# Layer norm from early moments, two weight units prepared ahead, and products that nobody reads

## The reference

```
def layernorm(x, g, b):
    mu = jnp.mean(xf, -1, keepdims=True)
    var = jnp.mean(jnp.square(xf - mu), -1, keepdims=True)
    return ((xf - mu) * lax.rsqrt(var + LN_EPS) * g + b).astype(x.dtype)

x = layernorm(ALPHA * x + part(x), g, b)        # four times, ALPHA = sqrt(2), LN_EPS = 1e-5
swiglu = (silu(x @ wg) * (x @ wu)) @ wd         # wg, wu: 1024 x 2816, wd: 2816 x 1024
```

## Time and profile before

| what | value |
|---|---|
| three runs shown | 1865.67, 1865.85, 1878.34 us, median 1865.85 |
| the profiled execution | 1866.61 us, of it the span of the core 1865.0 us |
| mean granted clock of TensorE | 0.926 of full speed |
| PE busy | 1659.9 us, 89% of the span |
| PEld, DVE, ACT, POOL busy | 81%, 40%, 35%, 13% |
| moved by DMA | 132.40 MB, mean 71 GB/s |

### The profile page before, as it was taken

One profiled execution on the slowest core, in us unless ns is written; L12 is line 12 of the kernel. 1 busy time (PEld: TensorE's weight loads), 2 busy tenths in 40 slices (PEclk: granted clock), 3 DMA queues, 4 the chain that ended last, 5 costly groups with the idle time before them and its releaser, 6 DMA issues. The chain is left out here.

```text
span 1865.0 us, 31270 instructions
## 1 busy us (share of the span) xinstructions
PE 1659.9 (89%) x12319; PEld 1511.7 (81%) x12321; DVE 750.9 (40%) x1433; ACT 648.4 (35%) x1274; POOL 241.7 (13%) x345
## 2 busy tenths in 40 slices
PE   8995297889999899979956899998687999998996
PEld 7994167789999899869945567766587999998994
DVE  4325963443333322265336554443435333332224
ACT  4424262242222211165326554454315222221113
POOL 1002530110000000010042333331021000000000
PEclk9997598889999999989978699999798999999998
DMA  6332102213223233133342121001312233223321
GB/s 158 91 80 55 31 1 70 67 57 90 82 86 90 76 94 93 40 59 88 83 130 58 46 79 57 1 1 42 96 55 63 87 90 90 84 74 96 91 62 48
DMA packets 253288, 132.40 MB, mean 71 GB/s; under 512 B 45142, under 2 KB 252106, under 8 KB 253002
## 3 DMA queue, kind: packets, MB, share of 16 engines
q1 hardware_dynamic: 251402, 127.39, 24.6%
q0 software_dynamic: 1792, 3.76, 0.7%
HBM read 124.81 MB, written 10.43 MB: 73 GB/s over the span
## 5 line engine op out<-in xcount | busy, mean ns | idle before, releaser
L210 PE MATMUL ps<-x_hi,w_hi 128*128 128x272 f32 x2288 | 476.2, 289 | 4.6 <-DVEq L575 4.2
L214 PE MATMUL ps<-x_hi,w_lo 128*128 128x272 f32 x2288 | 474.9, 289 | 0.0
L212 PE MATMUL ps<-x_lo,w_hi 128*128 128x272 f32 x2288 | 473.2, 288 | 0.0
L227 DVE TENSOR_TENSOR w_lo<-w_raw,w_hi 128x1024 fp32r<-128x1024 f32 (+1 forms) x167 | 226.3, 1355 | 491.5 <-ACT w_hi L220 491.5
L220 ACT ACTIVATE w_hi<-w_raw 128x1024 fp32r<-128x1024 f32 (+1 forms) x179 | 199.8, 1116 | 640.6 <-PE ps L214 633.9
L210 PEld LDWEIGHTS ps<-x_hi,w_hi 128*128 128x128 f32 x2288 | 361.0, 189 | 7.0 <-DVEq L575 4.8
L212 PEld LDWEIGHTS ps<-x_lo,w_hi 128*128 128x128 f32 x2288 | 361.0, 189 | 0.0
L214 PEld LDWEIGHTS ps<-x_hi,w_lo 128*128 128x128 f32 x2288 | 358.7, 190 | 0.0
L210 PE MATMUL ps<-h_hi,w_hi 128*128 128x272 f32 x704 | 147.9, 292 | 9.7 <-DVEq L785 9.7
L214 PE MATMUL ps<-h_hi,w_lo 128*128 128x272 f32 x704 | 147.5, 291 | 0.0
L212 PE MATMUL ps<-h_lo,w_hi 128*128 128x272 f32 x704 | 147.1, 291 | 0.0
(11 more groups left out here) (392 smaller groups left out, 2052.7 us busy)
## 6 DMA issues: line engine op xcount, KB each, us to landing
w_raw<-in_ffn_w_gate SPq DMA_DIRECT2D x44, 512.0 KB, 3.8
w_raw<-in_ffn_w_up SPq DMA_DIRECT2D x44, 512.0 KB, 3.8
w_raw<-in_ffn_w_down SPq DMA_DIRECT2D x32, 704.0 KB, 4.7
w_raw<-in_ab_w_in SPq DMA_DIRECT2D x17, 512.0 KB, 4.2
w_raw<-in_c_w_in SPq DMA_DIRECT2D x13, 512.0 KB, 3.8
w_raw<-in_c_w_in SPq DMA_DIRECT2D x16, 256.0 KB, 3.9
w_raw<-in_c_w_out SPq DMA_DIRECT2D x32, 128.0 KB, 3.1
w_raw<-in_ab_w_in SPq DMA_DIRECT2D x10, 256.0 KB, 4.8
```

Source lines behind the costliest of these rows:

```text
L210: pe.matmul(out, c.w_hi[:, slot, k, :], x_hi[:, k0 + k, cols], start=first, stop=False)
L212: pe.matmul(out, c.w_hi[:, slot, k, :], x_lo[:, k0 + k, cols], start=False, stop=False)
L214: last = pe.matmul(out, c.w_lo[:, slot, k, :], x_hi[:, k0 + k, cols], start=False, stop=end)
L227: return dve.tensor_tensor(c.w_lo[:, slot, 0:kt, :], c.w_raw[:, slot, 0:kt, :], c.w_hi[:, slot, 0:kt, :].bitcast(F32), ALU.subtract)
```

## The change

Four things are altered together.

**Moments early.** `Moments` runs in `stage_out_proj` and `stage_ffn_down`. After the second tile PE forms a mean of tile 0 (`pe_level`, two products), ACT stores it times 8 as `shift`, and DVE subtracts it from each tile: from tiles 0 and 1 after their adds, from the others ahead of theirs (divided by ALPHA). So the sums stay small. POOL adds tile and square to `x_sum` and `sq_sum`; ACT squares each tile as it comes; DVE makes the two last additions; PE turns the sums into moments per token, 8 chunks of 68 tokens each (`pe_tokens`, one column per product).

**Norm on small tiles.** Variance, root and reciprocal are taken on 68 x 8. PE spreads the reciprocal back over the partitions with 8 products into banks 4 and 5, after the two products of the mean. DVE centres and scales tile by tile, with the spread root read from PSUM.

**Two units ahead.** Both first units of the next stage are loaded in the stage before; slot 0 is split there, slot 1 at the start of the norm. `pe_first_pair` works on both: tiles 0 to 2 for both, then the rest of the first, then tiles 3 to 7 of the second. It also replaces `pe_first_unit` in the opening stage.

**Products that nobody reads.** `keep_running` adds 3 products of 272 columns before the moments and 5 after the spread.

Beside these, `stage_out_proj` uses three pairs of banks in place of four, the lists of `stage_ffn_down` on DVE, ACT, SP and POOL are written out instead of looped, and `sq_sum` and `shift` serve as buffers in the attention stages.

```diff
+def pe_first_pair(c, pe, start):
...
     for k in range(KT):
         start.wait_tile(pe, k)
+        first = products(0, k)
+        if k < SHARED:                       # SHARED = 3
+            products(1, k)
+    for k in range(SHARED, KT):
+        second = products(1, k)
+    return first, second

+def keep_running(c, pe, bank, n):
+    for i in range(n):
+        pe.matmul(c.ps[:, bank + i % 2, 0:HALF], c.k("mean"), c.const[:, 0:HALF], start=True, stop=True)

+class Moments:
...
+    def dve_after_add(self, dve, n):
+        if n == 1:
+            self.dve_move(dve, 0)
+            self.dve_move(dve, 1)
+        if 1 <= n < KT - 1:
+            self.dve_move_early(dve, n + 1)
+    def pool_sums(self, pool):
+        for n in range(1, KT - 1):
+            self.sum_x(pool, n)
+            self.sum_sq(pool, n)
+    def dve_last_sums(self, dve):
+        self.sum_x(dve, KT - 1)
+        self.sum_sq(dve, KT - 1)
+    def pe_tokens(self, pe, x, at):
+        for i in range(CHUNKS):              # 8 chunks of TOK = 68
+            pe.matmul(c.ps[0:TOK, STAT, at + i:at + i + 1], x[:, i * TOK:(i + 1) * TOK], c.k("mean")[:, 0:1], ...)
+    def pe_moments(self, pe):
+        keep_running(self.c, pe, MEAN, 3)
+        pe.wait_ge(self.x_summed, KT - 1)
+        self.pe_tokens(pe, self.c.x_sum, 0)
+        pe.wait_ge(self.sq_summed, KT - 1)
+        self.pe_tokens(pe, self.c.sq_sum, CHUNKS)

 class Norm:
     def pe(self, pe):
+        last = pe.matmul(c.ps[:, MEAN + h, 0:HALF], c.k("mean"), c.x_sum[...])        # h = 0, 1
+        pe.wait_ge(self.inverted, 1)
+        for i in range(CHUNKS):
+            last = pe.matmul(c.ps[:, ROOT + h, o:o + TOK], self.rstd[:, i:i + 1].broadcast_to([TOK, P]), c.k("ident")[0:TOK, 0:TOK], ...)
+        last.then_inc(self.spread, 1)
+        keep_running(c, pe, 0, 5)
     def dve(self, dve, split=None):
+        dve.tensor_tensor(self.var[:, :], e2, self.m2[:, :], ALU.subtract).then_inc(self.var_set, 1)
+        dve.reciprocal(self.rstd[:, :], self.std[:, :]).then_inc(self.inverted, 1)
+        centre(0)
+        if split:
+            split(1)
+        centre(1)
         for k in range(KT):
+            scale(k)
+            if k + 2 < KT:
+                centre(k + 2)
+            if split and k % 2 == 0:
+                self.low(dve, k)
     def act(self, act, split=None):
+        act.activation(self.m2[:, :], c.ps[0:TOK, STAT, 0:CHUNKS], ACT.Square).then_inc(self.m2_set, 1)
+        act.activation(self.std[:, :], self.var[:, :], ACT.Sqrt, bias=c.eps[0:TOK, :]).then_inc(self.rooted, 1)
+        if split:
+            split(1)
+            for k in range(KT):
+                shift(c.x_hi[:, k, :], k).then_inc(self.hi, 1)
+                if k % 2 == 1:
+                    shift(c.xT[:, k, :], k).then_inc(self.done, 1)
             for k in range(0, KT, 2):
                 shift(c.xT[:, k, :], k).then_inc(self.done, 1)

 def stage_in_proj(...):
             def _(pe):
                 start.pe(pe)
-                pe.wait_ge(lo_made, 1)
-                pe_first_unit(c, pe, start).then_inc(unit_used, 1)
+                pe.wait_ge(lo_made, 2)
+                for last in pe_first_pair(c, pe, start):
+                    last.then_inc(unit_used, 1)
                 start.pe_late(pe, 6)

 def stage_out_proj(...):                      # ACT; stage_ffn_down has the same pattern
+                for n in range(KT):
+                    if 2 <= n + 1 < KT:
+                        split_hi(c, act, (n + 1) % 2, KT).then_inc(hi_made, 1)
+                    if n == KT - 1:
+                        ahead.split_hi(act, 0)
+                    if n == 1:
+                        moments.act_level(act)
+                        moments.act_square(act, 0)
+                    if n:
+                        moments.act_square(act, n)
+                moments.act_ready(act)
```

More of the change, by code:

```diff
@@ L124, in setup_memory @@
     c.xT = sb("xT", [P, KT, T])
-    c.x_sum = sb("x_sum", [P, T])
+    c.x_sum, c.sq_sum, c.shift = (sb(n, [P, T]) for n in ("x_sum", "sq_sum", "shift"))
+    c.eps = sb("eps", [P, 1])
     c.x_hi = sb("x_hi", [P, KT, T], F32R)
@@ L191, in pe_first_unit, with products @@
-def pe_first_unit(c, pe, start):
+        split_lo(self.c, dve, slot, self.units[slot][1], self.scale)
+SHARED = 3
+def pe_first_pair(c, pe, start):
+    def products(slot, k):
+        for h in range(2):
+            cols = slice(h * HALF, (h + 1) * HALF)
+            out = c.ps[:, 2 * slot + h, 0:HALF]
+            pe.matmul(out, c.w_hi[:, slot, k, :], c.x_hi[:, k, cols], start=k == 0, stop=False)
+            pe.matmul(out, c.w_hi[:, slot, k, :], c.x_lo[:, k, cols], start=False, stop=False)
+            last = pe.matmul(out, c.w_lo[:, slot, k, :], c.x_hi[:, k, cols], start=False, stop=k == KT - 1)
+        return last
@@ L193, in pe_first_unit @@
     for k in range(KT):
         start.wait_tile(pe, k)
-        for h in range(2):
-            cols = slice(h * HALF, (h + 1) * HALF)
-            out = c.ps[:, h, 0:HALF]
-            pe.matmul(out, c.w_hi[:, 0, k, :], c.x_hi[:, k, cols], start=k == 0, stop=False)
-            pe.matmul(out, c.w_hi[:, 0, k, :], c.x_lo[:, k, cols], start=False, stop=False)
-            last = pe.matmul(out, c.w_lo[:, 0, k, :], c.x_hi[:, k, cols], start=False, stop=k == KT - 1)
-    return last
+        first = products(0, k)
@@ L391, in dve, with scale @@
+        def scale(k):
+            dve.wait_ge(self.spread, 1)
+            dve.wait_ge(self.centred, k + 1)
+            dve.scalar_tensor_tensor(halves(c.xT[:, k, :]), halves(c.xT[:, k, :]), c.ln_gb[:, self.which, 0, k:k + 1],
+                                     c.ps[:, ROOT:ROOT + 2, 0:HALF], ALU.mult, ALU.mult).then_inc(self.scaled, 1)
         dve.wait_ge(self.rooted, 1)
         dve.reciprocal(self.rstd[:, :], self.std[:, :]).then_inc(self.inverted, 1)
-        dve.wait_ge(self.inverted, 1)
@@ L394, in dve @@
-        dve.wait_ge(self.squared, KT)
-        for k in range(KT):
-            dve.scalar_tensor_tensor(c.xT[:, k, :], c.xT[:, k, :], c.ln_gb[:, self.which, 0, k:k + 1], self.rstd[:, :],
-                                     ALU.mult, ALU.mult).then_inc(self.scaled, 1)
-            if split and k >= 2 and k % 2 == 0:
-                self.low(dve, k - 2)
-        if split:
-            self.low(dve, KT - 2)
+        dve.wait_ge(self.mean_set, 1)
+        centre(0)
+        if split:
+            split(1)
@@ L1234, in stage_attend_prompt @@
         sb = lambda n, s: tmp.enter_context(nc.sbuf_tensor(f"{name}_{n}", s, F32))
-        prob = sb("prob", [P, n_prob, SEQ])
+        prob_own = sb("prob", [P, n_prob - 2, SEQ])
+        prob = [prob_own[:, i, :] for i in range(n_prob - 2)] + [c.sq_sum[:, 0:SEQ], c.shift[:, 0:SEQ]]
         probT = sb("probT", [P, n_probT, NB, P])
```

451 lines of the change are left out of this document (258 added, 193 removed).

## The result

The changed kernel took 1846.68 us (median of 4 runs, 1844.46 to 1857.75), the kernel before 1866.78 on the same chip: a ratio of 0.9882, 95% interval 0.9842 to 0.9923: 1.2% faster, and the interval leaves out no change. The forecast was 1846.

The account below looks back on a forecast made before the run. TensorE idles around each norm as engines take turns. Norms gain 32.8, less 3.4 (pe_level), 0.8 (out_proj) and 7.4 (opening): 21.2 off 1866.6 gives 1845.4, called 1846 us; range 1839 to 1853.

Parts of the forecast that it names:

- Tail: End of the stage before a norm: sums, moment products (0.08 a row) and meeting put the norm's start at T + 5.5.
- Head of the norm: Norm's start: spread at full clock (1.8; 3.8 at half), tile 0 scaled at 4.35; 1.0 taken for a fallen clock.
- rival B: Given-back gain: clock sags at DVE's pace (8.1) or POOL's second sum holds out_proj's split (7.0); 1854, chance 0.25.
- Tiles: Norm's tile loop: DVE stands for POOL, 4.25 for two tiles; centring and scaling run beside POOL; both units done at 26.8.
- in_proj: Norm ahead of in_proj: PE stands 2.9 until slot 0 holds a unit again, so 5.5 of 8.4 remain.
- Store: Norm before the store, no splits: ScalarE's last tile at T + 18.7 against 27.2, a gain of 8.5.
- Costs: Elsewhere: pe_level's two products 0.85 in four stages, 3.4; out_proj's split for unit 3 late by 0.4, twice, 0.8.
- B's second half: In out_proj: POOL's second sum holds the split in each of five units for 0.7, twice, 7.0.
- Opening: Opening stage: the pair waits for the second split (19.7); unit 2 starts at 37.7 instead of 30.32, costing 7.4.
- The 2.0 for a clock that must rise first: Opening pair: 2.0 on top of 12.0 for 96 products, bounds 1.1 and 3.1.
- Rival C: Norms and opening: unread products fail, the clock falls at the meeting's 1.1 rest and stays at half; 1885, chance 0.08.
- Rival A: Norms: more overlap, DVE doesn't stand for POOL, a moment row costs 0.04, the clock holds; 1832, chance 0.15.

Follow-up runs that it names:

- the combined kernel: Changed kernel, but opening with one unit, x_lo of all tiles by DVE, every tile shared in norms, late work reordered: 1825.50 us, ratio 0.9763 to kernel before.

## Why the prediction was right

**Tail.** (T is the start of the last addition, as in the forecast.) The norm was to start at T + 5.5; measured 5.03. A row of the moment products costs 0.07, within the bounds and a little under the 0.08 taken. The three unread products were covered, and the meeting took 1.26.

**Head of the norm: the step that failed.** The forecast took full clock for the spread, and 1.0 for all that the clock might take. The clock fell at T + 3.5 in the first norm (the windows: 362.1), inside the moment products, and in the others at T + 5.2 (in the mean), 4.3 (in the rest at the meeting) and 6.4 (in the spread). In the first norm the mean took 2.15 and the spread 3.52, near the upper end of 3.8; tile 0 was scaled 6.28 behind the norm's start, not 4.35. The last 36 products took 6.5 in place of 4.5. That is 3.9 in place of 1.0, the size that stood in rival B. In the second trace of the same kernel it was 2.4. That it is the clock and not the row costs, the run with unread products between the moment products shows: in in_proj's norm, where its clock held, tile 0 was scaled 4.37 behind the norm's start, as forecast.

**Tiles.** Forecast: two tiles in 4.25, from tile 0 scaled to tile 7 scaled 15.0, then 2.9. Measured 15.07 and 2.97. DVE's `low` lasted 1.33 beside POOL, and the run in which POOL makes none brought it to 0.78. DVE did not stand for the whole of POOL's instruction: POOL was busy for 0.75 of the `low`, which became 0.55 longer. The forecast let centring run beside POOL, since it takes one operand from PSUM. In the first norm centring came first (373.45, POOL's `x_lo` at 373.85): it took 0.71 like all others and POOL its 1.35, but 0.3 of overlap is little. The changed kernel's second attention has a clearer pair, POOL working on two operands in SBUF while DVE starts behind it with one operand in PSUM and one in SBUF:

```profile
1088.24 0.62 POOL L1553 TENSOR_TENSOR sq_sum<-sq_sum,c_att_inv 128x256 f32<-128x256 f32 x1 [2.06 <-DVE c_att_inv L1521]
...
1088.61 0.27 DVE L1541 TENSOR_TENSOR x_lo<-ps,x_hi 128x128 fp32r<-128x128 f32 x1
```

DVE's 0.27 lies beside POOL for 0.25 of it, and neither is longer than usual (most of the 48 of that kind on DVE took 0.27, POOL's eight of that kind and size 0.61 to 0.62). So the sum was right to let centring run. The Trainium skill (SBUF — State Buffer, Who interferes with whom) says that a DVE instruction with at most one SBUF input, outside the 2-port perf modes, does not contend with GpSimd; the trace agrees, by this pair.

**in_proj.** A stand of 2.9 was forecast; it was 1.40 in one trace and 2.23 in another. PE came later itself: it was done with the pair 35.5 and 34.2 behind the last addition, where 33.3 was forecast. The 36.9 from last addition to third unit are what ScalarE's rewriting and rotary copies and DVE's turn and split make them; in the combined kernel, with the split taken ahead of the rotary work and the faster tiles, it was 29.1.

**Store.** ScalarE's last tile at T + 18.9 (1830.69 + 1.44), forecast 18.7; in the second trace, where the clock fell sooner, it came later, and the store gave 5.4 in place of 8.3.

**Costs.** `pe_level` cost 0.9 in each out_proj, as forecast. PE stood nowhere in out_proj, so the extra 0.4 there for the split of unit 3 was wrong; in up and down together 0.3 and 1.1 where 0.85 each was expected. Later units of out_proj kept 6.01: B's second half did not happen, because there DVE's split comes first and POOL's sum is what gets longer.

**Opening.** Third unit at 37.58, forecast 37.7, by two errors that met. The 2.0 for a clock that must rise first came from no row. The pair began at 18.99, 0.76 sooner than forecast, and was done at about 33.9: 14.9 in place of 14.0, with 0.43 a product until about 24.2 and 0.29 from then on, so that the term measured 2.9. Behind PE's rest of 3.71 the third unit ran at half in part, and by the third rotary turn the cost was 8.9.

**What made the total right.** The norms' shortfall (4.6) and the opening's (1.5) were met by 6.3 from the attention stages and 0.9 from cheaper levels. The forecast had no term for the attention, and no run shows that the change earns those 3.9 of the second one: the same code there took 503 to 510. So the sum was nearer than its steps deserved, and that nearness is luck. The 2.4 of the first attention came back in every kernel but the one that opens with one unit and keeps the old order; no term foresaw it. On the second trace of the changed kernel the norms gave 8.7 (first up) and 8.0, and the store 5.4.

**Rival C** was right that the unread products do not hold the clock, and wrong that it then stays at half. It came back 7 to 10 us after its fall in the four norms of the changed kernel; without unread products it came back 17 us after it in the three norms ahead of a unit and 24 in the store, in the combined kernel 10 to 14, and 21 in its store. PE made up for it before the last tile. **Rival A** needed DVE not to stand for POOL, and it stood. That the tiles come at DVE's pace and not at PE's is the likely reason why the unread products decide nothing: the stretches are alike within 0.1 with them and without.

## What to carry to other kernels

When a stage is bound by engines that take turns, find the engine that sets the pace of its tiles (here DVE, with POOL in its way) before buying anything for TensorE: eight products that nobody reads in each norm moved nothing, while giving `x_lo` to one engine, with the rewriting reordered for it, took 8.6 us off three norms. A new way of working need not be used everywhere it fits: sharing tiles between two units gains 5.7 us in three norms, where both weight units are ready early, and the pair loses 8.6 us in the opening stage, where the second is not (6.1 were left of it by out_proj). And judge a change of 1% by stretches of the trace that it touches as well as by the total, since unchanged stages here swing by 3 to 6 us with the clock.

## What the runs showed of the hardware

- Of DVE and POOL, where both read two tiles in SBUF, the one that came later got longer. In the earlier trace rows POOL's addition started 0.35 ahead of DVE's split, which took 2.08; in the changed kernel DVE's split started 0.09 ahead of POOL's sum and took its 1.23, and POOL's sum lasted 2.35. The delay was a little less than the overlap: 0.55 for a `low` that lay beside POOL for 0.75.
- A DVE instruction with one operand in PSUM and one in SBUF was not longer beside POOL (0.27 at 1088.61, as alone).
- The granted clock of TensorE dropped to the level of 1.2 GHz in the second attention of some kernels with PE busy all the time (0.65 over ten us), and not in others whose code there is the same (1.00). The stretch of about 505 us took 503 at a mean clock of 0.91 and 509 at 0.89.
- A product of 128x272 in fp32 that nobody reads cost 0.50 between the moment products, at full clock.
